# Feed-forward weights: low parts on one engine, two at a time and two units ahead

## The reference

```
h2 = rms_norm(x, g_ffn[l])
gt = causal_dwconv(h2 @ w_ffn_gate[l], ffn_conv_w[l])       # width 3
x = x + (jax.nn.silu(gt) * (h2 @ w_ffn_up[l])) @ w_ffn_down[l]
```

```
a, b = jnp.split(h @ w_up, 2, axis=-1)
return (jax.nn.silu(a) * b) @ w_down
```

## Time and profile before

| | |
|---|---|
| Median of 3 runs | 1911.15 us (1908.98 to 1918.33) |
| Profiled execution, its own time | 1914.11 us |
| its span, first to last instruction | 1912.3 us |
| mean granted TensorE clock | 0.965 of full |
| PE busy | 1804.9 us (94%), 13416 matmuls |
| DVE busy | 1174.4 us (61%) |
| ACT busy | 944.4 us (49%) |
| POOL busy | 318.0 us (17%), 64 of its 71 instructions low parts |
| DVE low parts (L437) | 213, 505.3 us, 2380 ns each |
| POOL low parts (L437) | 64, 316.8 us, 4951 ns each |
| ACT high parts (L429) | 277, 525.4 us, 1899 ns each |

### The profile page before, as it was taken

How to read it: one execution, slowest core, us unless ns; L and a number is a source line. 1 busy time by engine, 2 the same in 40 slices (tenths; PEclk the granted TensorE clock), 3 DMA queues, 4 the chain that set the end, 5 groups by cost and what they waited for, 6 DMA issues and landing times.

```text
span 1912.3 us, 31649 instructions
## 1 busy us (share of the span) xinstructions
PE 1804.9 (94%) x13416; PEld 1691.9 (88%) x13416; DVE 1174.4 (61%) x1864; ACT 944.4 (49%) x1298; POOL 318.0 (17%) x71
## 2 busy tenths in 40 slices
PE   7999999989999999999999978799999978899998
PEld 7989999989889999998998877669998977779986
DVE  6976666666459767666664657556454734555453
ACT  5445564534455465645444545454334654454332
POOL 2611100345427120004355000000000000000000
PEclk9899999999999999999999989689999999899999
DMA  7684445545546644454555463124556644234562
GB/s 232 168 229 133 155 147 186 175 155 179 218 138 181 194 146 147 154 194 154 177 177 198 138 178 111 67 67 133 176 184 226 180 141 129 89 111 155 177 219 79
DMA packets 249148, 305.75 MB, mean 160 GB/s; under 512 B 9778, under 2 KB 224142, under 8 KB 249007
## 3 DMA queue, kind: packets, MB, share of 16 engines
q1 hardware_dynamic: 235959, 289.66, 47.2%
q10 hardware_dynamic: 13048, 14.07, 3.6%
HBM read 299.51 MB, written 4.19 MB: 159 GB/s over the span
## 4 chain that ended last, share of the span: by engine, by line
PE 66%; DVE 13%; ACT 8%; DMA 7%; issue 3%; ACTq 1%; POOL 0%; DVEq 0%; SPq 0%; POOLq 0%
PE psum L461 20%; PE psum L462 19%; PE psum L463 19%; DVE wlo L437 6%; ACT whi L429 4%; DMA raw<-in_b_w_q 2%; DMA raw<-in_w_in 2%; DMA raw<-in_a_w_in 1%; DVE hT L615 1%; ACTq L2454 1%; DMA raw<-in_b_w_out 1%; DMA raw<-in_ffn_w_up 1%; ACT work L2030 1%; ACT hidden L901 1%; PE psum L2397 1%
## 5 line engine op out<-in xcount | busy, mean ns | idle before, releaser
L429 ACT ACTIVATE whi<-raw 128x2048 fp32r<-128x2048 f32 (+2 forms) x277 | 525.4, 1899 | 318.2 <-PE psum L463 164.5
L461 PE MATMUL psum<-hT,whi 128*128 128x256 f32 x2160 | 621.2, 288 | 16.9 <-DVE wlo L437 16.9
L437 DVE TENSOR_TENSOR wlo<-raw,whi 128x2048 fp32r<-128x2048 f32 x213 | 505.3, 2380 | 193.8 <-PE psum L463 151.0
L462 PE MATMUL psum<-hT,whi 128*128 128x256 f32 x2160 | 615.2, 285 | 0.0
L463 PE MATMUL psum<-hT,wlo 128*128 128x256 f32 x2160 | 614.8, 285 | 0.0
L437 POOL TENSOR_TENSOR wlo<-raw,whi 128x2048 fp32r<-128x2048 f32 x64 | 316.8, 4951 | 743.1 <-PE psum L463 535.7
L461 PEld LDWEIGHTS psum<-hT,whi 128*128 128x128 f32 x2160 | 418.3, 194 | 24.2 <-DVE wlo L437 21.7
L462 PEld LDWEIGHTS psum<-hT,whi 128*128 128x128 f32 x2160 | 418.5, 194 | 0.2
L463 PEld LDWEIGHTS psum<-hT,wlo 128*128 128x128 f32 x2160 | 418.2, 194 | 0.0
L461 PE MATMUL psum<-whi,hT 128*128 128x256 f32 (+2 forms) x448 | 145.2, 324 | 1.1 <-issue 1.1
L462 PE MATMUL psum<-wlo,hT 128*128 128x256 f32 (+2 forms) x448 | 144.3, 322 | 0.0
(11 more groups left out here) (353 smaller groups left out, 2856.0 us busy)
## 6 DMA issues: line engine op xcount, KB each, us to landing
raw<-in_w_in SPq DMA_DIRECT2D x78, 1024.0 KB, 5.9
raw<-in_ffn_w_up SPq DMA_DIRECT2D x44, 1024.0 KB, 5.2
raw<-in_w_ffn_gate SPq DMA_DIRECT2D x22, 1024.0 KB, 5.4
raw<-in_w_ffn_up SPq DMA_DIRECT2D x22, 1024.0 KB, 5.3
raw<-in_w_ffn_down SPq DMA_DIRECT2D x22, 1024.0 KB, 4.9
raw<-in_ffn_w_down SPq DMA_DIRECT2D x22, 1024.0 KB, 5.1
raw<-in_b_w_q SPq DMA_DIRECT2D x12, 1024.0 KB, 5.2
raw<-in_a_w_in SPq DMA_DIRECT2D x10, 1024.0 KB, 5.3
```

The costliest lines, as they stand in the source:

```text
L429: act.activation(part(whi, n, HIGH_SLOTS), part(raw, n, RAW_SLOTS), ACT.Copy).then_inc(high_made, 1)
L437: eng.tensor_tensor(part(wlo, n, LOW_SLOTS), part(raw, n, RAW_SLOTS), part(whi, n, HIGH_SLOTS).bitcast(F32), ALU.subtract).then_inc(stream ...
L461: nc.tensor.matmul(dst, left[0], right[0], start=first, stop=False)
L462: nc.tensor.matmul(dst, left[0], right[1], start=False, stop=False)
```

## The change

Four things change, all in the feed-forward blocks.

First, every low part of the feed-forward weights is DVE's. Before, in the first part of the network, gate units, the first up unit and every other down unit were POOL's.

Second, in an up stage DVE now makes two low parts directly behind each `product(c)`: those of units 2c+3 and 2c+4. Before, DVE's low parts stood in two places of a pair, one of them between `low(c - 1)` and `product(c)`.

Third, ACT makes high parts one unit sooner: in pair c it makes unit 2c+4 before the silu and unit 2c+5 behind it, then `high(c)` of the same pair. Before, it was units 2c+2 and 2c+3, and `high(c - 1)`.

Fourth, with a convolution, the gate product from pair 2 on is copied out of PSUM by DVE, not ACT. `gate_scaled` is now signalled for every pair, with an empty instruction on DVE. The two tensors `hT` become two halves of one tensor at the same place. `small_ready` is declared and used by nothing.

The core of the diff:

```diff
         for c in range(FT // 2):
-            u += [(a["w_ffn_gate"][l][:, c * S:(c + 1) * S], "P"), (a["w_ffn_up"][l][:, c * S:(c + 1) * S], "PV"[c > 0])]
-        u += row_units(a["w_ffn_down"][l], FT, "PV")
+            u += [(a["w_ffn_gate"][l][:, c * S:(c + 1) * S], "V"), (a["w_ffn_up"][l][:, c * S:(c + 1) * S], "V")]
+        u += row_units(a["w_ffn_down"][l], FT, "V")
...
                 def silu(c):
                     if conv is None:
-                        if 2 * c < RAW:
-                            act.wait_ge(gate_scaled.sem, gate_scaled.at(c + 1))
-                        ins = act.activation(cacc[:, c % 2], pair_of(2 * c), ACT.Silu)
+                        act.wait_ge(gate_scaled.sem, gate_scaled.at(c + 1))
+                        src = tiles(2 * c)
                     else:
                         act.wait_ge(operand_ready.sem, operand_ready.at(c + 1))
-                        ins = act.activation(cacc[:, c % 2], cacc[:, c % 2], ACT.Silu)
-                    ins.then_inc(inner_ready.sem, 1)
+                        src = cacc[:, c % 2]
+                    act.activation(cacc[:, c % 2], src, ACT.Silu).then_inc(inner_ready.sem, 1)
...
                 for c in range(pairs):
-                    make_high(act, n0 + 2 * c + 3)
                     act.wait_ge(bank_full.sem, bank_full.at(2 * c + 1))
-                    if conv is None:
-                        if c >= 2:
-                            act.wait_ge(bank_free.sem, bank_free.at(2 * c - 2))
-                        silu(c)
-                        make_high(act, n0 + 2 * c + 4)
-                        if c:
-                            high(c - 1)
-                        continue
                     if c >= 2:
-                        act.wait_ge(operand_ready.sem, operand_ready.at(c - 1))
-                    if 2 * c >= RAW:
-                        act.activation(gpad[:, c % 2, :, pad:], pair_of(2 * c), ACT.Copy).then_inc(scores_ready.sem, 1)
-                    make_high(act, n0 + 2 * c + 4)
+                        act.wait_ge(bank_free.sem, bank_free.at(2 * c - 2))
+                    make_high(act, n0 + 2 * c + 5)
                     silu(c)
-                    if c:
-                        high(c - 1)
-                high(pairs - 1)
-                make_high(act, n0 + 2 * pairs + HIGH_SLOTS)
+                    make_high(act, n0 + 2 * c + 6)
+                    high(c)
...
+                def gate(c):
+                    dve.wait_ge(bank_full.sem, bank_full.at(2 * c + 1))
+                    dst = tiles(2 * c) if conv is None else gpad[:, c % 2, :, pad:]
+                    if 2 * c < RAW:
+                        v_link(dve.tensor_tensor(dst, tiles(2 * c), half(), ALU.mult))
+                    elif conv is not None:
+                        v_link(dve.tensor_copy(dst, tiles(2 * c)))
+                    nc.vector.nop().then_inc(gate_scaled.sem, 1)
...
                 for c in range(pairs):
-                    b = c % 2
+                    gate(c)
                     if c == 0:
-                        gate(0)
                         whole_rows(dve, turned)
-                    make_lows(dve, n0 + 2 * c + 2)
-                    if c == 1:
-                        gate(1)
                     if conv is not None:
...
-                    if c:
+                        short_conv(c)
+                    if c == 0:
+                        make_lows(dve, n0 + 4)
+                    else:
                         low(c - 1)
-                    make_lows(dve, n0 + 2 * c + 3 + (c == 0))
                     product(c)
                     if c == 0:
                         for b in range(4):
                             whole_low(dve, hT, turned, gain, b)
-                make_lows(dve, n0 + 2 * pairs + 2)
+                    make_lows(dve, n0 + 2 * c + 5)
                 low(pairs - 1)
                 end(dve)
```

More of the change, by code:

```diff
@@ L269, in over @@
             return nc.alloc_sbuf_tensor_at(name, [P] + shape, dt, offset=base + 4 * start)
-        hT = [over(f"hT{i}", at_h, i * KT * S, [KT, S]) for i in range(2)]
+        hT_both = over("hT", at_h, 0, [2, KT, S])
+        hT = [hT_both[:, i] for i in range(2)]
         ROWS = 32
@@ L351, in two_part_transformer @@
         gate_scaled = signal("gate_scaled")
+        small_ready = signal("small_ready")
         means_ready = signal("means_ready")
@@ L868, in _ @@
                     w = take_unit(pe, n0 + n)
-                    if n >= 4:
-                        pe.wait_ge(bank_free.sem, bank_free.at(n - 3))
-                    if n == 3:
-                        pe.wait_ge(root_spread.sem, root_spread.at(1))
-                    if n == RAW:
-                        whole_turned(pe)
+                    await_banks(pe, n)
                     if n == 0:
-                        mm = first_unit(pe, w, rows, [own(0)[:, j * S:(j + 1) * S] for j in range(2)], True)
+                        mm = first_unit(pe, w, rows, [bank(up)[:, j * S:(j + 1) * S] for j in range(2)], True)
                     else:
-                        mm = columns_product(pe, own(n), w, rows if n < RAW else hT)
+                        mm = columns_product(pe, bank(first_bank(n)), w, rows if n < RAW else hT)
                     mm.then_inc(bank_full.sem, 1)
@@ L934, in _, with short_conv @@
                 begin(dve)
+                half = lambda: spread(root_row[:, :], 1, 2)
+                def gate(c):
[6 more added lines that the diff above has]
+                    nc.vector.nop().then_inc(gate_scaled.sem, 1)
+                def short_conv(c):
+                    b = c % 2
+                    n = [0, 0]
+                    for k in range(SHORT):
+                        for j in range(2):
+                            src = gpad[:, b, j, k:k + S]
+                            if k == 0:
+                                ins = dve.tensor_scalar(cacc[:, b, j, :], src, conv(k, 2 * c + j), None, ALU.mult)
+                            else:
+                                v_wait(n[j])
+                                ins = dve.scalar_tensor_tensor(cacc[:, b, j, :], src, conv(k, 2 * c + j),
+                                                               cacc[:, b, j, :], ALU.mult, ALU.add)
+                            n[j] = v_done(ins)
+                    v_wait(n[1])
+                    nc.vector.nop().then_inc(operand_ready.sem, 1)
                 def product(c):
+                    u = tiles(2 * c + 1)
                     dve.wait_ge(bank_full.sem, bank_full.at(2 * c + 2))
                     if 2 * c < RAW:
-                        up = pair_of(2 * c + 1)
-                        v_link(dve.tensor_tensor(up, up, spread(root_row[:, :], 1, 2), ALU.mult))
+                        v_link(dve.tensor_tensor(u, u, half(), ALU.mult))
                     dve.wait_ge(inner_ready.sem, inner_ready.at(c + 1))
```

50 lines of the change are left out of this document (16 added, 34 removed).

## The result

The changed kernel takes 1892.91 us (median of 6 runs, 1888.3 to 1893.69) against 1912.0 us (6 runs) of the kernel before: ratio 0.9896, interval 0.9871 to 0.9921. That is 19.1 us faster; 21.9 were forecast, 1889.2 with a range of 1885 to 1902. Two more sets of runs of the same file gave 0.9892 (0.9864 to 0.992) and 0.9899 (0.9873 to 0.9924).

A forecast was written before the change was run, and what follows sets the result against it. The prediction saw PE as the main engine, waiting for late low parts in four up stages: 24.3 us excess less 2 x 1.2 residue is 21.9, so 1911.15 - 21.9 = 1889.2 us, range 1885 to 1902.

The forecast's parts named there:

- The excess of 24.3 us: Four up stages: time in all beyond 120.5 us a stage without waits, the most the change can remove.
- Step 1: Second part's up stages, from the third pair: DVE's low parts come in time, nine waits of 0.34 us a stage go.
- Step 2: Raw buffer ring: loop of 11.0 us against PE's 11.52 closes with landings up to 5.7 us; nothing charged in second part.
- Step 3: First part: POOL's 36 low parts go to DVE, busy about 9 of 11.52 us; low parts return to 2.29 us.
- Step 4: Start of second part's up stages: the 1.72 us wait before unit 4 goes, with 0.8 us to spare.
- Step 5: Start of first part's up stages: 0.9 us wait stays, 0.3 added for unit 7; residue 1.2 us each in two stages.
- Step 6: Merge stage and down stages: moved low parts and extra DVE waits and empty instructions cost 0.
- The sum: Four up stages: 24.3 - 2 x 1.2 = 21.9 us saved; 1892.2 us for a profiled execution, 1889.2 for the median.
- (c): Rival, chance 0.07: slower, raw buffer ring becomes the bound from landings of about 6.9 us; 1942 us at 7.5.
- (a): Rival, chance 0.13: small waits stay in the up stages, half the gain, 12 us; 1899 us.
- (b): Rival, chance 0.08: no change, something else paces, such as the ring at landings of 6.7 us; 1911 to 1913 us.

The follow-up runs named there:

- e4: Changed kernel with unit 5's low part made directly behind unit 4's, not behind product 1, in all four up stages: 1885.02 us, ratio 0.9893 to the kernel before.
- e3: Changed kernel with DVE's low parts back in their places of before, ACT's new order kept: ratio 1.0004 to the kernel before.
- e2: Changed kernel with ACT's order of high parts as before, DVE's new order kept: ratio 1.0159 to the kernel before.
- e6: Changed kernel with one extra DVE instruction between product and low parts, third and fourth up stage, from pair 1: 1907.33 us.
- e7: Changed kernel with two extra DVE instructions between product and low parts, third and fourth up stage, from pair 1: 1929.01 us.
- e11: Changed kernel run again with nothing changed: 1892.49 us, ratio 0.9899 to the kernel before.
- e1: Kernel before with only the feed-forward low parts all given to DVE, both orders as before: ratio 1.0153 to the kernel before.
- e9: Changed kernel with POOL's feed-forward low parts as before, all orders new: ratio 1.0199 to the kernel before.

## Why the prediction was right, step by step

- **The excess of 24.3 us over 120.5 us a stage.** Right: 120.4 us is what a stage without waits takes in both the changed kernel and e4 (119.8 where the early matmuls are 0.113 us apart, as they were in the second stage of before).
- **Step 1, steady state of the second part.** Right: 120.4 us, no wait. But the prediction credits DVE's order; e3 shows that ACT's order alone removes the small waits, and e2 that DVE's alone does, too, and leaves one before unit 5. (They were eight, before units 6 to 20, with 0.1 us each for the restart; the tenth wait of the earlier trace rows stands before unit 22, behind the stage. The excess, read from the windows, is not touched by the miscount.) Either is enough in the second part.
- **Step 2, the ring.** Right for the second part and confirmed by e6 and e7: a loop of 11.1 us with 1.24 or 2.48 us more is 0.8 or 2.1 us too long, 7.4 and 18.5 us in nine pairs, where 7.3 and 6.7, and 18.3 and 18.2, were measured. The landing of the second transfer of a pair was mis-sized, 6.0 to 6.8 us in the median where I took 5.5 from one group of three. It cost nothing, since the loop hangs on the first. What the prediction did not work out is the loop of the first part. There the first landing takes 5.4 us, and the fetches of gate units in the second stage follow each other by 11.3 to 11.5 us: it has at most 0.2 us a pair to spare. Low parts of odd units from 7 to 19 come there 0.05 to 1.3 us before PE wants them, in the second part 0.4 to 2.3, so a single late landing can make PE wait in the first part; in the second part of the changed kernel none did, with landings up to 7.35 us.
- **Step 3, POOL's low parts to DVE.** DVE's load of 9 us a pair was right, and 2.29 us each. What the sum did not say is how much hangs on the three parts together. By runs against before: letters alone +1.5%, letters with DVE's order +1.6%, letters with ACT's order 0.0%, both orders with POOL's letters +2.0%, all three -1.0%. Of the four incomplete versions none is a gain in the first part: its stages take 130 to 148 us there, against 127.2. One order alone with POOL's letters was not run.
- **Step 4, start of the second part's stages.** Right: 1.72 us before unit 4 are gone.
- **Step 5, start of the first part's.** The step that was mis-sized: 0.9 us before unit 5 and 0.3 before unit 7, 1.2 a stage. Measured in the first stage 1.7, 1.1 and 0.5 us before units 5, 7 and 15, in the second 1.1 before unit 5; over 120.4 us the stages are 3.0 and 1.2 us long (in the first, early matmuls 0.6 us faster offset a part). The low part of unit 5 came when foretold (it ended 2.29 us after 378.83, where the working gives 381.0 in this execution's time), but PE reached unit 5 0.6 us sooner, because the matmuls of units 1 to 3 were 0.113 us apart there, where the first stage of before had 0.118 (142 of them make 0.6 us). In e11, where they were 0.118 apart again, the wait before unit 5 is 1.06 us, close to the 0.9. The rest are late landings on the loop, of 6.73 and 6.37 us for units 8 and 16, which the 0.3 us for unit 7 did not cover.
- **Step 6.** Right: the three stretches between the up stages differ by 0.1, 0.0 and 0.7 us in the two profiles.
- **The sum.** 21.9 forecast for the stages, 20.5 measured in the profile and 20.5 to 21.3 over three profiles. The medians differ by 19.1, 19.6 and 19.4 us; the remaining 1 to 2 us lie within the interval. That the profiled execution came out at 1888.3 us, 4 under the 1892.2 forecast for it, is luck: the short landing ahead of the first stage gave 5.5.

Of the rivals, (c) is the one that the runs price: with landings as they are it did not come, but it was nearer than it was put: 1.24 us more in the loop cost 7 us a stage in e6, which in four stages would be more than the whole gain, where (c) asked for a landing 1.7 us longer. (That a later landing costs what a later low part costs is argued, not run.) (a) and (b) fall, as no small wait stays in the second part.

## What to carry to other kernels

When two engines hand work back and forth once per pair, add up each loop through both of them, waits included, and compare it with the bound engine's time: a part of such a change alone can put the partner's old order, or a slower instruction, into the loop and lose more than the whole change gains, as e1, e2 and e9 did. Slack of a result is not slack of the buffer it frees: e6 added 1.2 us where the result was mostly ready 1.2 us or more ahead, and lost 7 us a stage. When two engines slow each other, look at which one starts first (e9). Compare stages by the starts of the same matmul, not spans: here 5 us of the difference between two profiles was one transfer far ahead of the change.

## What was not expected of the hardware

- The second of two 1 MB transfers issued 2.2 us apart lands in 6.0 to 6.8 us in the median of a stage, the first in 5.1 to 5.5; single first ones took up to 7.35 us. Issued 0.4 us apart (e9), the second takes 7.7 to 9.3 us.
- Of two low parts at once on DVE and POOL, the one that starts second waits out the first almost whole (e9).
- One transfer issued near 122 us lands in 12.2 to 13.6 us in some executions and in 5.8 to 6.5 in others, also of the same file. In all thirteen it is long exactly where ACT's write of 768 KB was issued ahead of it.
- Matmuls of units 1 to 3 of a stage, which read the rows without the norm's factor, are 0.118 us apart in some stages of some executions and 0.113 in others, later ones always 0.120, all at a clock of 1.00. That alone is 0.6 us a stage. The cause is open.
